# Which engine makes the low parts of the streamed weights in a two-layer encoder trunk on one core

## The reference, cut to what matters

```python
for layer in range(2):
    x = x + 0.5 * swiglu(rms_norm(x, g1), wg1, wu1, wd1)      # 1024 -> 2816 -> 1024
    h = rms_norm(x, gm)
    if layer == 0:
        x = x + hyena_attention_mixer(h, ...)                 # one projection in, FFT convolution
                                                              # and windowed attention, one projection out
    else:
        x = x + rwkv7_bidir_mixer(h, ...)                     # six mixes of h, projections r, k, v and LoRAs,
                                                              # a scan in both directions, group norm, projection out
    x = x + 0.5 * swiglu(rms_norm(x, g2), wg2, wu2, wd2)

def swiglu(x, w_gate, w_up, w_down):
    return (jax.nn.silu(x @ w_gate) * (x @ w_up)) @ w_down
```

## Time and profile before

| what | value |
|---|---|
| time, median of 3 executions (lowest to highest) | 1450.52 us (1450.5 to 1456.49) |
| the profiled execution's own time | 1453.78 us |
| its span | 1452.0 us |
| PE busy | 1340.5 us (92%) |
| DVE busy | 875.2 us (60%) |
| ACT busy | 651.0 us (45%) |
| POOL busy | 517.2 us (36%) |
| L197 on POOL | 115 instructions, 382.9 us |
| L190 on DVE | 114 instructions, 248.2 us |

### The profile page before, as it was taken

The page is one execution under the profiler, slowest core; times in us unless marked ns, Lnnn a source line. Parts: engine busy times, 40 slices in busy tenths (PEclk is TensorE's granted clock), DMA queues, the critical chain, the costliest instruction groups (busy, mean ns, idle before and its releaser), DMA issues.

```text
span 1452.0 us, 32669 instructions
## 1 busy us (share of the span) xinstructions
PE 1340.5 (92%) x13902; PEld 1209.0 (83%) x13902; DVE 875.2 (60%) x1225; ACT 651.0 (45%) x1051; POOL 517.2 (36%) x264
## 2 busy tenths in 40 slices
PE   5999998999899999999985979789998998999998
PEld 3799998878799998899985976788888887889997
DVE  6465555786667655776657782555555525476664
ACT  4444555452555455545544565332322223445543
POOL 1144343211334432443432850443333302244442
PEclk9999999999999999999997996799999997999999
DMA  7255553323355455445542530000000021445543
GB/s 308 74 187 177 189 197 131 131 88 131 131 189 201 173 190 199 175 174 189 201 174 80 182 131 1 2 3 3 4 3 4 4 90 44 174 174 185 203 175 116
DMA packets 18238, 188.25 MB, mean 130 GB/s; under 512 B 2016, under 2 KB 2528, under 8 KB 3040
## 3 DMA queue, kind: packets, MB, share of 16 engines
q1 hardware_dynamic: 18144, 186.84, 35.4%
HBM read 185.78 MB, written 1.05 MB: 129 GB/s over the span
## 4 chain that ended last, share of the span: by engine, by line
PE 80%; DVE 12%; ACT 4%; issue 2%; DMA 0%; DVEq 0%; SPq 0%; ACTq 0%
PE gu_bank L248 22%; PE gu_bank L250 11%; PE gu_bank L1174 6%; PE bank L228 6%; PE bank L229 6%; PE bank L230 6%; PE bank L1155 5%; PE gu_bank L228 3%; PE gu_bank L230 3%; PE gu_bank L229 3%; PE gu_bank L1155 2%; DVE WL L190 2%; ACT WH L183 1%; PE gu_bank L312 1%; DVE raw L1493 1%
## 5 line engine op out<-in xcount | busy, mean ns | idle before, releaser
L197 POOL TENSOR_TENSOR WL<-raw,WH 128x1024 fp32r<-128x1024 f32 (+1 forms) x115 | 382.9, 3329 | 657.2 <-ACT WH L184 657.2
L248 PE MATMUL gu_bank<-HX,WH 128*128 128x512 f32 x1408 | 506.6, 402 | 9.6 <-DVE HX L338 7.9
L250 PE MATMUL gu_bank<-HX,WL 128*128 128x256 f32 x1408 | 397.1, 282 | 0.0
L190 DVE TENSOR_TENSOR WL<-raw,WH 128x2048 fp32r<-128x2048 f32 (+2 forms) x114 | 248.2, 2177 | 162.7 <-ACT WH L183 162.2
L248 PEld LDWEIGHTS gu_bank<-HX,WH 128*128 128x128 f32 x1408 | 266.9, 190 | 74.6 <-issue 12.4
L250 PEld LDWEIGHTS gu_bank<-HX,WL 128*128 128x128 f32 x1408 | 268.4, 191 | 0.3 <-issue 0.2
L183 ACT ACTIVATE WH<-raw 128x2048 fp32r<-128x2048 f32 (+2 forms) x115 | 208.6, 1814 | 30.1 <-PE gu_bank L230 14.4
L228 PE MATMUL bank<-PH,WH 128*128 128x256 f32 x704 | 199.6, 284 | 4.9 <-DVE PL L399 4.7
L229 PE MATMUL bank<-PL,WH 128*128 128x256 f32 x704 | 199.3, 283 | 0.0
L230 PE MATMUL bank<-PH,WL 128*128 128x256 f32 x704 | 199.2, 283 | 0.0
L228 PEld LDWEIGHTS bank<-PH,WH 128*128 128x128 f32 x704 | 133.6, 190 | 10.3 <-issue 6.4
(11 more groups left out here) (278 smaller groups left out, 2155.0 us busy)
## 6 DMA issues: line engine op xcount, KB each, us to landing
raw<-stream_in SPq DMA_DIRECT2D x114, 1536.0 KB, 6.7
cst<-const_in SPq DMA_DIRECT2D x1, 1568.0 KB, 17.0
X<-xT_in SPq DMA_DIRECT2D x1, 1024.0 KB, 5.3
raw<-stream_in SPq DMA_DIRECT2D x1, 1024.0 KB, 7.4
arena<-hconst_in SPq DMA_DIRECT2D x2, 512.0 KB, 10.7
out<-X SPq DMA_DIRECT2D x1, 1024.0 KB, 3.8
arena<-hconst_in SPq DMA_DIRECT2D x1, 768.0 KB, 13.8
arena<-fw_in SPq DMA_DIRECT2D x1, 512.0 KB, 8.1
```

Of the source, the lines that this page charges most:

```text
L190: nc.vector.tensor_tensor(WL[:, slot, :cut], raw[:, slot, :cut], WH[:, slot, :cut].bitcast(fp32), ALU.subtract).then_inc(lo_ready, 1)
L197: nc.gpsimd.tensor_tensor(WL[:, slot, cut:end], raw[:, slot, cut:end], WH[:, slot, cut:end].bitcast(fp32), ALU.subtract).then_inc(lo_last, 1)
L248: nc.tensor.matmul(out[:, :], WH[:, slot, w:w + P], HX[:, k, :, :].rearrange("p i t -> p (i t)"), start=k == 0, stop=False)
L250: last = nc.tensor.matmul(out[:, L:2 * L], WL[:, slot, w:w + P], HH[:, k, :], start=False, stop=k == CT - 1)
```

## The change

`split_lo` on DVE makes the whole low part of a step, in two instructions: the first part as before, then, after a wait for `hi_last`, the last part, which adds to `lo_last`. The steps of the output projection behind the scan (S_O to S_O + 3) return before the second; theirs stay with POOL. At the first step after them (S_FFN[3]) DVE also waits until POOL's are done, so that `lo_last` counts in order. `pool_ffn` goes, and with it every `split_last` in `pool_mix0` and `pool_mixes`; POOL keeps its gates, its two mixes and its work in the scan.

```diff
         def split_lo(dve, s, slot=None):
             slot = s % 2 if slot is None else slot
-            cut, _ = parts(s)
+            cut, end = parts(s)
             dve.wait_ge(hi_ready, s + 1)
             nc.vector.tensor_tensor(WL[:, slot, :cut], raw[:, slot, :cut],
                                     WH[:, slot, :cut].bitcast(fp32), ALU.subtract).then_inc(lo_ready, 1)
+            if isinstance(s, int) and S_O <= s < S_FFN[3]:
+                return
+            dve.wait_ge(hi_last, s + 1)
+            if isinstance(s, int) and s == S_FFN[3]:
+                dve.wait_ge(lo_last, s)
+            nc.vector.tensor_tensor(WL[:, slot, cut:end], raw[:, slot, cut:end],
+                                    WH[:, slot, cut:end].bitcast(fp32), ALU.subtract).then_inc(lo_last, 1)
...
-        def pool_ffn(pool, s0):
-            p0 = s0 % 2
-            split_last(pool, s0)
-            split_last(pool, s0 + 1)
-            with pool.Fori(0, (FT - 2) // 2) as i:
-                for u in range(2):
-                    split_last(pool, s0 + 2 * i + (2 + u), slot=(p0 + u) % 2)
-            split_last(pool, s0 + FT)
...
-            for s in range(4):
-                split_last(pool, S_IN + s)
-            gate(0)
-            split_last(pool, S_IN + 4)
-            gate(1)
-            split_last(pool, S_IN + 5)
-            gate(2)
-            gate(3)
-            for s in range(S_OUT, S_FFN[1]):
-                split_last(pool, s)
+            for c in range(HT):
+                gate(c)
...
-            split_last(pool, S_RKV)
...
-                    if k % 3 == 2:
-                        split_last(pool, S_RKV + 1 + 4 * n + k // 3)
...
-                    if k % 4 == 3:
-                        split_last(pool, S_RKV + 3 + 4 * n + k // 4)
-            split_last(pool, S_LORA + 1)
...
-            pool_ffn(pool, S_FFN[0])
             pool_mix0(pool)
-            pool_ffn(pool, S_FFN[1])
-            pool_ffn(pool, S_FFN[2])
             pool_mixes(pool)
...
-            pool_ffn(pool, S_FFN[3])
```

## The result

The changed kernel takes 1457.7 us (median of 6 executions, 1457.14 to 1459.9) against 1451.32 for the kernel before beside it (6 executions, 1449.52 to 1456.49). The ratio is 1.0039 with a 95% interval of 1.0021 to 1.0058: some 5.7 us slower (3.0 to 8.4). The forecast was 1453, in a range of 1446 to 1461.5, within 0.5% with a chance of 0.83. The profiled execution has 1459.9 us and a span of 1458.1, against 1453.78 and 1452.0: 6.1 us in both.

A forecast was written before the change was run, and what follows sets the result against it. PE was taken to bound the kernel, standing still mainly at entries waiting for DVE. Terms 5.51 - 2.02 + 0.35 - 1.5 gave +2.3 us on the median 1450.52: 1453 us, range 1446 to 1461.5.

The forecast's parts named there:

- Steady steps: Within the feed-forward loops: DVE's added 1.14 us is offset as L394 falls to 0.69 us; PE hides it, so nothing.
- Entries: At five stage entries DVE's added instruction delays the residual: 4 x 1.14 + 0.95, +5.5 us.
- The clock at the entries: Half-speed stretches of PE behind its idle at the five entries; the forecast's sum added nothing for them.
- rival (b): Each of five entries gets one more half-speed stretch, 1.75 us each: +11 in all, 1461.5 us; chance 0.17.
- Start: In the filter's second round L603 is no longer stalled by POOL's split of step 0: -2.0 us.
- Mixers: First mixer +0.35 us (evacuation 0.65, softmax -0.3); mixes of the second mixer -1.5 us, from shorter PE waits.
- Rival (a): Added instructions find cover at the entries, only the stalls matter: -3.8 us, 1447 us; chance 0.13.
- Rival (c): Another phase spares most of the 20 us at half speed behind the scan, some 6 us: 1446.5 us; chance 0.07.
- the forecast's own band: The whole kernel's change lies between -1 and +6 us, around +2.3; chance 0.6.

The follow-up runs named there:

- loops: The kernel before, with DVE making the last parts within the four feed-forward stages alone, not at their first steps: ratio 1.0004 (0.9989 to 1.0020).
- entries: The kernel before, with DVE making the last part at the five entry steps alone: ratio 1.0053 (1.0035 to 1.0070), +7.7 us.
- fill: The changed kernel, with matmuls that nobody reads put in PE's idle stretch at the five entries: ratio 0.9965, 1448.24 us.
- start: The kernel before, with DVE making the last part of step 0 alone: ratio 1.0004 (0.9988 to 1.0021).
- mixers: The kernel before, with DVE making the last parts within the two mixers alone, not at their first steps: ratio 0.9985 (0.9969 to 1.0000), -2.2 us.
- fill_scan: The changed kernel, with filling matmuls at the entries and six more at the start of the output projection behind the scan: ratio 0.9932, 1443.43 us.
- before_fill_scan: The kernel before, POOL splitting as it did, with filling matmuls alone at the entries and six behind the scan: ratio 0.9922, 1444.9 us.

## Why the prediction was right, and where its sum was off

- **Steady steps at nothing.** Right. `loops` has 1.0004, and between the second step and the end of the second and third stage the traces differ by -0.11 and +0.02 us. The reason was right too: L394 fell from 1.87 to 0.69 us, and from L190's start to L394's end are 5.32 us in place of 5.11, 0.2 more for a wait for ACT, which PE's work covers.
- **Entries, +5.5 us of idle.** Right to the tenth: 1.14, 1.13, 0.96, 1.13, 1.13, with 0.96 at the third stage, where the 0.19 us that DVE waited for PE had been seen in the earlier trace rows. The figure of the Trainium skill (VectorE: DVE Perf Modes, "The TRN2 errata") would have made it 6.1: the length of the instruction is 1.22 or 1.23 in the trace, as that formula has it, but what it holds the path for is 1.14.
- **The clock at the entries, at nothing in the forecast: the step that failed, in its size.** It stood as rival (b), with 1.75 us for each of five stretches, 1461.5 us in all, and a chance of 0.17. All five came, and they cost 0.9 to 1.4 us each, 5.6 in sum. The price was too high since in a part of such a stretch PE waits for DVE anyway: at the first mixer's entry the clock fell 1.8 us before PE had work again. The argument against it, that entries with such a stretch "come back in 3.5 us", took the length in one execution for the entry's own; at the same idle it was 0, 3.4 or 6.8 us in others. That all five came in the profiled execution is in part luck: in `entries` four did, and over all profiles the longer idle brought 13 us more of half speed, not 17, which by the prices above is an estimated 4 us rather than 5.6. The section "HAM oscillation" of the Trainium skill's TensorE: Matmul & The Clock Gate has an array left idle fall back to half speed each time. The trace of the changed kernel agrees in all five entries, the third stage's included, and `fill` shows the idle as the cause; that of `loops` does not at the second stage, where 3.15 us of idle were followed by full speed.
- **Start, -2.0 us.** A row of one execution taken for the kernel's habit. The stall was in two of six profiled executions, and `start` alone gained nothing (-1.7 to +3.0 us). The fall in L603's time was read rightly; that it is worth 2 us in the median was not.
- **Mixers.** +0.35 and -1.5 us were forecast, -1.2 together; `mixers` measured -2.2 (-4.5 to 0). The single waits came as worked out: 0.57 for 0.65 at the evacuation, the 2.05 of the earlier trace rows down to 1.04, the wait for L190 gone. The remaining 1.2 us of gain in the mixes goes with a half-speed stretch that was shorter, and the scan, where nothing changed, took 1.53 us more, with 78.5 us at half speed in place of 71.7: no experiment ties these two to the change.
- **Rival (a), that entries find cover.** Wrong: the chain has DVE's L190, L197 and the residual back to back, and `entries` costs 7.7 us.
- **Rival (c).** Not what the change did (its stretch behind the scan is as long as before), but a true cost of this kernel: six filling products left 6.6 of the 20 us at half speed in `fill_scan`, and none in `before_fill_scan` (1.00 from 1210 to 1240 us).

So the mechanism at the entries and in the loops was right, and the size was off by the clock and by a start that is not gained on the median. The time lies within the range because rival (b), with its chance of 0.17, set the upper end; of the forecast's own band, -1 to +6 us on the median of 1450.5, the top is 1456.5, and 1457.7 was measured. In the profiled execution the +5.6 of clock was also partly met by gains elsewhere. One is not the change's: the -1.2 in the first stage goes with 3.4 us at half speed near 40 us in place of 6.8, and `mixers` and `loops`, where POOL makes step 0, have the 3.4 as well. The -0.9 in the output projection was not explained. The direction was right with too small a size: +2.3 forecast, +5.7 measured. Open: how much of the +5.7 would be there over many more executions; the kernel before spreads over 9 us by itself, the changed one over 3.

## What to carry to other kernels

Where the busiest engine waits at the entry of a stage, an instruction added ahead of what it waits for costs the time that it holds its engine for, and on TensorE it may cost as much again in clock: read the granted clock of each entry, before and after, and in more than one execution, since the same entry differs between them. Filling such a wait with products that nobody reads, sized to end before the real work can start, was worth more here (0.8%) than moving the low parts between engines. Take from one profiled execution only what doesn't hang on when a DMA lands.

## What the runs showed of the hardware

A short idle of PE costs twice where it ends at half speed, and 1.1 us more of it could be enough. At the third stage's entry PE idled 1.6 us in its longest wait and kept full speed, in all seven profiled executions with the short idle and no fill; at 2.6 us it came back with 3.4 us at half speed, in both with the long one. Elsewhere it varied: behind 3.1 to 4.0 us of idle half speed lasted mostly 3.4 us, but also 6.8 and once nothing, and behind 4.3 to 5.1 us it lasted 6.8 us in seven entries of eight.

The executions of the kernel before lie between 1449.3 and 1458.3 us over all the comparisons, with nothing changed. In one set of 30, the 14 with a mean clock of 0.951 or 0.952 took 1449.46 to 1452.52 us and the 7 with 0.945 or 0.946 took 1454.84 to 1457.47: most of this kernel's spread goes with TensorE's clock.

A VectorE instruction with two operands that takes 1.22 us holds the next one up for 1.13 or 1.14 us only: 839.66 to 840.79 in the mixes.

A stall by POOL can hang on which of two engines starts first, where neither waits for the other: a split that began 0.57 us later than L603 left it at 0.28 us, and so did one that began 0.02 us later (`mixers`); one that began 0.18 us ahead of it made 2.3 us of it.
